# An encoder block on one core: 40 instead of 32 tokens by gathered rows, one-hot tiles shared by GpSimd and ACT, two dots in each body of the spread

## The reference

```python
q = (t @ w_pq).reshape(n_tok, PEER_HEADS, 2, PEER_QDIM // 2)
sc = jnp.einsum('thcd,hckd->thck', q, sub_keys)
top_s, top_i = lax.top_k(sc, PEER_TOPK)
...
best_s, best_j = lax.top_k(cand_s, PEER_TOPK)
expert_idx = jnp.take_along_axis(cand_i, best_j, axis=-1)
gate = jax.nn.softmax(best_s, axis=-1)
...
a = gelu(einsum('thkd,td->thk', expert_u[ib], tb))
vv = expert_v[ib]
return jnp.einsum('thk,thkd->td', (gb * a), vv)
```

## Time and profile before

| | |
|---|---|
| median of 3 runs | 2143.06 us (2139.74 to 2143.27) |
| the profiled execution | 2139.2 us, span 2137.2 us |
| granted clock of TensorE | 0.997 of full speed in the mean |
| busy in the span | PE 99%, PEld 92%, DVE 74%, ACT 52%, POOL 23% |
| moved by DMA | 482.26 MB, 226 GB/s |
| stages in the span | "u" from about 775 to 1470, in it the spread 1017 to 1344; "down" to 2125 |

### The profile page before, as it was taken

The page is one execution under the profiler, slowest core; times in us unless marked ns, Lnnn a source line. Parts: engine busy times, 40 slices in busy tenths (PEclk is TensorE's granted clock), DMA queues, the critical chain, the costliest instruction groups (busy, mean ns, idle before and its releaser), DMA issues.

```text
span 2137.2 us, 40878 instructions
## 1 busy us (share of the span) xinstructions
PE 2108.7 (99%) x13494; PEld 1973.4 (92%) x13494; DVE 1584.1 (74%) x2622; ACT 1118.9 (52%) x1879; POOL 488.8 (23%) x379
## 2 busy tenths in 40 slices
PE   8999999999999999999999999999999999999997
PEld 6888888889989999999999999999999999999997
DVE  6555566667777986888778888888777776777775
ACT  5444455446455655556555555555555554555553
POOL 0000000000000000001999999332222220111110
PEclk9999999999999999999999999999999999999998
DMA  7655554445556556666767666888877776877773
GB/s 246 235 187 190 183 166 157 149 155 189 181 192 230 166 174 210 207 210 224 228 221 222 222 221 222 286 309 313 312 286 291 285 283 215 267 275 266 268 251 128
DMA packets 134750, 482.26 MB, mean 226 GB/s; under 512 B 15455, under 2 KB 18399, under 8 KB 134295
## 3 DMA queue, kind: packets, MB, share of 16 engines
q1 hardware_dynamic: 116072, 414.29, 57.6%
q0 software_dynamic: 18432, 67.12, 8.8%
q10 hardware_dynamic: 174, 0.05, 0.0%
HBM read 477.16 MB, written 4.24 MB: 225 GB/s over the span
## 4 chain that ended last, share of the span: by engine, by line
PE 95%; DVE 3%; issue 1%; DMA 1%; ACT 0%; DVEq 0%; SPq 0%; ACTq 0%
PE ps L1643 35%; PE ps L1912 19%; PE ps L1650 19%; PE ps L1916 11%; PE ps L1673 5%; PE ps L1896 2%; DVE lo L1014 1%; PE ps L1767 1%; PE ps L1749 1%; PE ps L1758 0%; DMA raw<-w_down 0%; DMA x_t<-x_t 0%; DVE score_b L1322 0%; DVE idx_now L1324 0%; DVE top_now L1328 0%
## 5 line engine op out<-in xcount | busy, mean ns | idle before, releaser
L1014 DVE TENSOR_TENSOR lo<-raw,hi 128x1024 fp32r<-128x1024 f32 x760 | 935.3, 1231 | 473.5 <-PE ps L1643 144.5
L622 ACT CAST hi<-raw 128x1024 fp32r<-128x1024 f32 x760 | 795.7, 1053 | 346.8 <-DMA raw<-w_down 137.6
L1643 PE MATMUL ps<-move_u,hi 128*128 128x448 f32 x2048 | 451.1, 368 | 0.0
L1912 PE MATMUL ps<-act_now,hi 128*128 128x448 f32 x2048 | 439.8, 365 | 0.4 <-ACT hi L622 0.4
L1912 PEld LDWEIGHTS ps<-act_now,hi 128*128 128x128 f32 x2048 | 375.0, 188 | 26.4 <-issue 0.7
L1643 PEld LDWEIGHTS ps<-move_u,hi 128*128 128x128 f32 x2048 | 371.0, 189 | 24.6
L1643 PE MATMUL ps<-move,hi 128*128 128x512 f32 x1536 | 379.3, 395 | 9.5 <-ACT hi L622 9.5
L1643 PEld LDWEIGHTS ps<-move,hi 128*128 128x128 f32 x1536 | 281.5, 189 | 62.9 <-issue 9.5
L630 ACT COPY upper<-ps 128x224 f32<-128x224 f32 (+1 forms) x224 | 80.3, 358 | 484.3 <-PE ps L1643 484.2
L602 POOL TENSOR_SCALAR one_j<-iota,j_t,gate_t 128x128 f32<-128x128 f32 x224 | 296.8, 1331 | 3.0 <-ACT j_t L880 1.8
L1916 PEld LDWEIGHTS ps<-act_now,lo 128*128 128x128 f32 x2048 | 250.6, 191 | 7.3 <-DVE lo L1014 2.0
(11 more groups left out here) (206 smaller groups left out, 1628.2 us busy)
## 6 DMA issues: line engine op xcount, KB each, us to landing
raw<-w_u SPq DMA_DIRECT2D x256, 512.0 KB
raw<-w_down SPq DMA_DIRECT2D x256, 512.0 KB
raw<-w_qk SPq DMA_DIRECT2D x68, 512.0 KB
raw<-w_gate SPq DMA_DIRECT2D x64, 512.0 KB
raw<-w_out SPq DMA_DIRECT2D x32, 512.0 KB
raw<-w_pq SPq DMA_DIRECT2D x32, 512.0 KB
raw<-w_v SPq DMA_DIRECT2D x28, 512.0 KB
raw<-w_o SPq DMA_DIRECT2D x24, 512.0 KB
```

Source lines behind the costliest of these rows:

```text
L622: nc.scalar.copy(hi[slot][:], raw[slot][:]).then_inc(hi_ready, 1)
L1014: nc.vector.tensor_tensor(lo[s % LOS][:], raw[s % RAW][:], hi[s % RAW][:].bitcast(F32), ALU.subtract).then_inc(lo_ready, 1)
L1643: ins = nc.tensor.matmul(ps[bank][:, 0:2 * w], hi[slot][:, col:col + P], m, start=begins, stop=ends)
L1912: return nc.tensor.matmul(ps[d][:, 0:2 * TD], hi[s % RAW][:, d * P:(d + 1) * P], act_now[s % ACTS][:], start=begins, stop=ends)
```

## The change

S goes from 32 to 40 tokens, so TD from 224 to 216: the wide matmuls of "u" and "down" have 432 moving columns instead of 448, the narrow ones 216 instead of 224, and there are 108 pairs instead of 112 (UG = 51). COPIES is 3 (120 partitions used), PICKS 43, STEPS 86. The `rows` ring has 3 buffers. Dots stand at s = 3 in bodies 22 and 23 and at s = 1 and 3 from body 24 on, so the last is in body 65. Additions start at chunk 16, 2.55 chunks apart, in the second half at chunk 2, 2.88 apart. POOL makes only the first `one_j` tile of a pair; ACT makes the second in two activations, Square of (iota - j) into `far` and Relu of (gate - gate * far), four pairs ahead. `sel` is three matrices, and the selection six matmuls. `fold` is loaded later, behind `move_free`.

```diff
-S = 32
+S = 40
 TD = T - S
 COPIES = P // S
-PICKS = PH * TOPK // COPIES
+NP = COPIES * S
+PICKS = -(-PH * TOPK // COPIES)
+ROWS = 3
 STEPS = 2 * PICKS
...
-WEIGHED = (STEPS - (UG - UR) - 2 * (CHUNKS["u"] // BODY - UG) + 1) // 2
+DOT_AT = [it * BODY + s for it in range(UR, (CHUNKS["u"] + CHUNKS["down"]) // BODY) for s in (1, 3)
+          if s == 3 or it >= U0][:STEPS]
+WEIGHED = DOT_AT[-1] // BODY + 1 - CHUNKS["u"] // BODY
...
+def row_before_pair(n):
+
+    return tuple(g for g in range(2, STEPS) if DOT_AT[g] < UG * BODY and max(0, DOT_AT[g] - U0 * BODY - 2) == n)
...
-    first, apart = (2, 7 / 2) if half else ((WEIGHED + 2) * BODY, 11 / 4)
+    first = 2 if half else (WEIGHED + 2) * BODY
+    apart = (HALF * BODY - 5 - first) / (PICKS - 1)
...
             sp.wait_ge(move_free, 1)
+            sp.dma_start(fold[:], A["fold"]).then_inc(fold_in, 16)
...
-                if table == "u_rows" and n >= 2:
-                    pool.wait_ge(dot_done, n - 1)
-                if table == "w_down":
-                    pool.wait_ge(dot_done, min(STEPS, STEPS - 1 + n))
-                    if n >= 2:
-                        pool.wait_ge(row_added, n - 1)
+                g = n + STEPS * (table == "w_down")
+                if ROWS <= g:
+                    pool.wait_ge(dot_done, min(STEPS, g - ROWS + 1))
+                if ROWS + STEPS <= g:
+                    pool.wait_ge(row_added, g - ROWS - STEPS + 1)
...
             for n in range(PAIRS):
-                if n % BODY == 2:
-                    gather("u_rows", n // BODY + 2)
+                for g in row_before_pair(n):
+                    gather("u_rows", g)
                 if n >= 2 * TOGETHER:
                     pool.wait_ge(gates_spread, n - 2 * TOGETHER + 1)
-                for t in (2 * n, 2 * n + 1):
-                    ins = nc.gpsimd.tensor_scalar(one_j[n % 4][:, t % 2, :], iota128[:], j_t[:, t:t + 1], gate_t[:, t:t + 1],
-                                                  ALU.is_equal, ALU.mult)
-                ins.then_inc(one_j_ready, 1)
+                nc.gpsimd.tensor_scalar(one_j[n % 4][:, 0, :], iota128[:], j_t[:, 2 * n:2 * n + 1], gate_t[:, 2 * n:2 * n + 1],
+                                        ALU.is_equal, ALU.mult).then_inc(one_j_ready, 1)
...
+            def second_one(n):
+
+                t = 2 * n + 1
+                if n:
+                    a.wait_ge(second_ready, n)
+                nc.scalar.activation(far[:], iota128[:], ACT.Square, bias=j_t[:, t:t + 1]).then_inc(far_ready, 1)
+                a.wait_ge(far_ready, n + 1)
+                nc.scalar.activation(one_j[n % 4][:, 1, :], far[:], ACT.Relu, bias=gate_t[:, t:t + 1], scale=neg_g[:, n:n + 1]
+                                     ).then_inc(second_ready, 1)
...
+                if n + 2 * TOGETHER < PAIRS:
+                    second_one(n + 2 * TOGETHER)
...
+                        pe.wait_ge(second_ready, n + (m + 1))
...
+            for it in range(UG - (UG - U0) % 2, UG):
+                body("u", it, before=spread_gates((it - U0) % 2))
```

More of the change, by code:

```diff
@@ L366, in build @@
         e_pair = at("e_pair", ARENA + 98 * KB, [P, 2, P])
-        sel = at("sel", ARENA + 99 * KB, [P, P])
-        rows = [at(f"rows{i}", ARENA + (112 + 4 * i) * KB, [P, CW]) for i in range(2)]
+        sel = at("sel", ARENA + 96 * KB, [P, COPIES, P])
+        rows = [at(f"rows{i}", ARENA + (112, 116, 108)[i] * KB, [P, CW]) for i in range(ROWS)]
         acc = at("acc", ARENA + 120 * KB, [P, D])
         idx = at("idx", MOVE + 31 * KB, [P, STEPS], U32)
[L371 to L374, removed]
+        dots = at("dots", MOVE + 31 * KB + 352, [P, STEPS])
+        gates_s = at("gates_s", MOVE + 31 * KB + 704, [P, PICKS])
+        w_s = dots[0:NP, 0:PICKS]
+        fold = at("fold", MOVE + 16 * KB + 2 * TD * 4, [P, S])
         x2 = at("x2", MOVE, [P, KT, T])
@@ L861, in gelu_and_index @@
                     a.wait_ge(e_turned, 1)
[L862 to L867, removed]
+                    nc.scalar.copy(idx[:], ps[7][:, 0:STEPS])
+                    nc.scalar.copy(gates_s[0:NP, :], ps[7][0:NP, 2 * P:2 * P + PICKS]).then_inc(idx_ready, 1)
             for first, tt in ((1, 1), (EXP_AT[1] + 1, 0)):
@@ L879, in gelu_and_gates @@
                     nc.scalar.copy(gate_t[:], ps[4][:, 0:T]).then_inc(experts_ready, 1)
-                    nc.scalar.copy(j_t[:], ps[6][:, 0:T]).then_inc(experts_ready, 1)
+                    even, odd = (ps[6][:, 0:T].rearrange("p (n u) -> p u n", u=2)[:, u, :] for u in range(2))
+                    nc.scalar.copy(j_t[:].rearrange("p (n u) -> p u n", u=2)[:, 0, :], even)
+                    nc.scalar.activation(j_t[:].rearrange("p (n u) -> p u n", u=2)[:, 1, :], odd, ACT.Copy, scale=-1.0
+                                         ).then_inc(experts_ready, 1)
+                    nc.scalar.activation(neg_g[:], ps[4][:, 0:TD].rearrange("p (n u) -> p u n", u=2)[:, 1, :], ACT.Copy, scale=-1.0
+                                         ).then_inc(experts_ready, 1)
+                    a.wait_ge(iota_ready, 2)
+                    a.wait_ge(experts_ready, 3)
+                second_one(s)
             body("u", INDEXED + 1, gelu_kept)
@@ L954, in gelu_w @@
                     a.wait_ge(w_summed, 1)
-                    nc.scalar.activation(w_s[:], w_s[:], ACT.Gelu).then_inc(w_gelu, 1)
+                    nc.scalar.activation(w_s, w_s, ACT.Gelu).then_inc(w_gelu, 1)
             def square_tile(d):
@@ L1449, in dot_of @@
             def dot_of(n):
[L1451 to L1454, removed]
+                v.wait_ge(row_landed[n % ROWS], 16 * (n // ROWS + 1))
+                c, row = n // PICKS * CW, rows[n % ROWS][0:NP, :]
+                nc.vector.tensor_tensor_reduce(row, row, h_rows[0:NP, c:c + CW], 1.0, 0.0, ALU.mult, ALU.add,
+                                               dots[0:NP, n:n + 1]).then_inc(dot_done, 1)
             def dots_at(it, s):
@@ L1553, in weights_at @@
                     v.wait_ge(idx_ready, 1)
[L1554 removed]
+                    nc.vector.tensor_tensor(w_s, w_s, gates_s[0:NP, :], ALU.mult).then_inc(w_ready, 1)
             def rows_at(it, s, half):
@@ L1870, in _ @@
             pe.wait_ge(e_ready, 1)
-            pe.wait_ge(sel_in, 16 * 2)
-            nc.tensor.matmul(ps[7][:, 0:2 * P], sel[:], e_pair[:].rearrange("p c k -> p (c k)"), start=True, stop=True)
-            nc.tensor.matmul(ps[7][:, 2 * P:3 * P], sel[:], found_g[:, 1, :], start=True, stop=True).then_inc(e_turned, 1)
+            pe.wait_ge(sel_in, 16)
+            own_of = [slice(q * PICKS, min((q + 1) * PICKS, P)) for q in range(COPIES)]
+            chosen = ps[7][:, 0:2 * PICKS].rearrange("p (c m) -> p c m", c=2)
+            for q, own in enumerate(own_of):
+                nc.tensor.matmul(chosen[:, :, 0:own.stop - own.start], sel[:, q, :], e_pair[:, :, own],
+                                 start=q == 0, stop=q == COPIES - 1)
+            for q, own in enumerate(own_of):
+                ins = nc.tensor.matmul(ps[7][:, 2 * P:2 * P + own.stop - own.start], sel[:, q, :], found_g[:, 1, own],
+                                       start=q == 0, stop=q == COPIES - 1)
+            ins.then_inc(e_turned, 1)
             with pe.Fori(INDEXED, UR + 1) as it:
@@ L2038, in columns, with own_copies @@
     return np.ascontiguousarray(b.reshape(-1, P, CW))
+def own_copies():
+    sel = np.zeros((P, COPIES, P), np.float32)
+    for q in range(COPIES):
+        sel[P - S:, q, q * S:(q + 1) * S] = np.eye(S, dtype=np.float32)
+    return sel
 def weave(wa, wb):
@@ L2061 @@
         "ident": np.eye(P, dtype=np.float32),
-        "sel": np.ascontiguousarray(np.tile(np.eye(P, dtype=np.float32)[:, P - S:], (1, COPIES))),
-        "fold": np.tile(np.eye(S, dtype=np.float32), (COPIES, 1)),
+        "sel": own_copies(),
+        "fold": np.pad(np.tile(np.eye(S, dtype=np.float32), (COPIES, 1)), ((0, P - NP), (0, 0))),
         "bias_rows": bias_rows(),
```

46 lines of the change are left out of this document (25 added, 21 removed).

## The result

The changed kernel takes 2124.61 us in the median of 5 runs (2121.91 to 2129.4), the kernel before 2143.05: a ratio of 0.9919 with an interval of 0.9903 to 0.9935. That is 17.4 us less by the ratio (18.4 by the two medians), where 27.8 were forecast. Its profiled span is 2123.2 us, 14.0 less than the 2137.2 of before; the profiled execution of before was a quick one (2139.2), that of the changed kernel was at its median (2124.97), so differences between the two traces come out 3 to 4 us smaller than those between medians.

A forecast was written before the change was run, and what follows sets the result against it. TensorE's own stream was taken as the bound (95% of the chain). -26.9 - 1.8 + 0.9 = -27.8 us gave 2111.4 from the profiled execution, 2115.3 from the median; 2113 was predicted between them, range 2103 to 2125.

The forecast's parts named there:

- The wide matmuls: In "u" and "down", 448 to 432 columns: 6.6 ns less each over 4096 matmuls, 26.9 us less, all on the path.
- The narrow ones: Narrow matmuls of "u" and "down", 224 to 216 columns: no gain taken, 8.3 us kept for the low end.
- rival A: Narrow matmuls shrink too, by their slope: 8.3 us more gain, 2105 us; chance 0.10.
- the floor by the one-column matmuls: On TensorE, matmuls with one moving column take 110 ns each, so narrow ones at 111.3 ns gain nothing.
- The spread: Spread of the gates in "u": two chunks take 5.81 us instead of 5.92, without TensorE waiting on one-hot tiles.
- rival B: VectorE sets the pace of the spread, losing 6 us, perhaps 5 more: 2119 to 2124 us; chance 0.13.
- C: VectorE keeps GpSimd from its one-hot tiles in the spread: about 2243 us, mostly near 2150; chance 0.05.
- D: Wide matmuls don't follow the column count: 2141 us; chance 0.02.
- the one on "down": 43 additions a half instead of 32 on VectorE, 14 us more work where it was busy 237 of 323: cost nothing.
- The step on gathers: 44 more gathers of 512 KB, 23 MB; DMA share in the rest of "u" from 0.88 to 0.90: cost nothing.
- The remaining sum: Besides wide matmuls: fewer pairs 1.8 us less, larger selection 0.9 us more, everything else nothing.
- ACT's two activations: ACT's one-hot tile in the spread: 0.30 us each, four a half body 1.2 us, with waits some 1.6; hidden, cost nothing.

The follow-up runs named there:

- the two even runs: Changed kernel with the additions in "down" at even chunks only: at every second chunk 2114.25 us (0.9874), at its own spacing 2114.41 us (0.9875).

## Why the prediction was right and wrong

**Right.** The wide matmuls: 6.2 ns for 16 columns where 6.6 were put, all of it on TensorE's path in "u". The narrow ones did not move (111.3 and 111.3 ns): rival A is out, and the floor by the one-column matmuls was real. The spread: two chunks take 5.82 us (5.81 forecast) in 49 of the 53 distances between one-hot groups, with no wait on a one-hot tile or on lo in the list, at 94% for VectorE where 95% or more was put. The last four take 5.93 to 6.07:

```profile
1316.59 1.05 PE L1932 MATMUL ps<-one_j,one_i 128*128 128x128 f32 x8
1322.66 1.05 PE L1932 MATMUL ps<-one_j,one_i 128*128 128x128 f32 x8
```

There VectorE is busy 44.00 of 44.00 us (1280 to 1324): it sets the pace, rival B in small. The prediction worked out that VectorE would lack 0.7 us over the last dozen half bodies, and held it to be covered; 0.65 us were lost, none of them in the list of waits. Rivals C and D did not come; C's mechanism is real, as the run with both tiles on GpSimd shows, and sharing took it away. No table load was added with Relu and Square.

**Wrong.** The step that failed is the one on "down": it put 22 more additions, and their gathers, at nothing. It looked at VectorE's share (237 of 323 us) and at the last addition, not at where in the pair of chunks the others fall. The step on gathers, also put at nothing, reasoned from a DMA share of 0.88 in late "u" without a gap of TensorE, and did not look at "down". In late "u" every dot stood at one phase; the additions at 2.55 and 2.88 chunks fall on even and odd steps in turn. What it cost is seen in the runs: 2124.6 against 2114.3 for the same work in the even phase, 10 us (11.4 us in "down" between the two traces), of which TensorE's list of waits shows 5.5. Most of the rest are waits shorter than the tails of matmuls that the profile counts as busy: the late starts at the odd chunks come to 10.6 us in the changed kernel and to 1.6 in the even one. The wide matmuls gave 6.2 ns each, so 25.4 us were due where 26.9 were put. The remaining sum holds: 2113 was forecast, and with additions at even chunks the kernel takes 2114.25.

**Sizes that were off, hidden here.** (Rows of ACT, then of GpSimd, from 1016 to 1332.) ACT's two activations take 0.40 and 0.50 us, not 0.30; four in a half body are 1.8 us instead of the 1.2 to 1.6 put. GpSimd's gather takes 1.74 us in the new spread, not 1.03, but its tiles are shorter (1.18 us in the mean).

```profile
L888 ACT ACTIVATE one_j<-far,gate_t,neg_g 128x128 f32<-128x128 f32 x104 | 51.5, 495 | 3.5
L886 ACT ACTIVATE far<-iota,j_t 128x128 f32<-128x128 f32 x104 | 41.9, 402 | 0.0
```

```profile
L612 POOL TENSOR_SCALAR one_j<-iota,j_t,gate_t 128x128 f32<-128x128 f32 x105 | 122.8, 1177 | 2.2
L594 POOL DMA_INDIRECT rows<-u_rows,idx x54 | 94.0, 1742 | 90.8 <-DVE dots L1479 90.4 <-issue 0.5
```

**Open.** The phase of the addition straight ahead is not the whole account. In the changed kernel 19 odd chunks, from the first addition of a half to its last, start their narrow matmuls over 0.06 us late. Of these 8 had an addition straight ahead of that lo; the other 11, which lost as much (3.9 us against 3.8), had one a step before or behind, at an even step. In the two even runs no odd chunk from the first addition of a half to its last is late. So odd additions may also disturb later chunks, by the loads or the gathers that they set off; that was not tested. How the loss divides between the gather's traffic and the addition's time at one and the same moment was not told apart further: each cures most of it alone. Why the odd phase costs less when it comes at every second chunk (2118.6) than with the kernel's own spacing (2121.2 odd, 2124.6 mixed) is not shown either; the runs of the last two overlap. No run places the additions of the kernel before at even chunks.

## What to carry to other kernels

Work that is hung into a pipeline at a fractional spacing falls on every phase of it, the worst among them; look which of the neighbouring deadlines is tight (here 1.0 us for the lo of odd chunks, 2.6 for even ones, by the lines from 1742 on), and place all of it ahead of the loose one. A share of busy time cannot tell that: both engines and the DMA had more room in "down" than in "u". And price a narrower matmul from rows at two widths and from the narrowest ones in the trace, for a floor under them.

## What the runs showed of the hardware that was not expected

Matmuls with 216, 224 and a single moving column, all on 128 fp32 columns of weights, start 110 to 111 ns apart. GpSimd's issue of a gather took 1.03 us in the spread of before, with one a body, and 1.74 in the changed kernel, with two. The number a body does not decide it: with two a body and both tiles on GpSimd it was 1.15.

```profile
L594 POOL DMA_INDIRECT rows<-u_rows,idx x52 | 59.9, 1151 | 16.8 <-DVE dots L1481 9.3 <-issue 7.5
```

A one-hot tile of GpSimd, 0.78 us by itself, took up to 3.6 us beside VectorE's dot and lo; with both tiles on GpSimd beside two dots a body the kernel took 57 us more than the changed one.
